# Latent attention: the low parts of the later queries and keys are subtracted on GpSimd instead of VectorE, between its key-sum additions

## The reference, cut to what matters

```python
q = (rms_norm(c_q, g_cq) @ w_uq).reshape(b, l, MLA_HEADS, MLA_QK)      # 64 + 32 columns a head
kv = (rms_norm(c_kv, g_ckv) @ w_ukv).reshape(b, l, MLA_HEADS, MLA_NOPE + MLA_V)
k = jnp.concatenate([k_nope, k_rope], axis=-1)
q = rope_tail(rms_norm(q, g_q_mla), cos, sin)
k = rope_tail(rms_norm(k, g_k_mla), cos, sin)
o_mla = blocked_causal_attention(pad_front(q), pad_front(k), pad_front(v_mla), MLA_QK ** -0.5)[:, PAD:]
```

## Time and profile before

| | us |
|---|---|
| median of 3 runs | 1716.3 |
| lowest and highest of them | 1715.48 and 1719.96 |
| the profiled execution, its own time | 1712.75 |
| span of the profiled execution | 1710.6 |
| TensorE busy | 1657.1 (97% of the span) |
| VectorE busy | 885.7 (52%) |
| ScalarE busy | 624.3 (36%) |
| GpSimd busy | 174.1 (10%) |

### The profile page before, as it was taken

One profiled execution on the slowest core, in us unless ns is written; L12 is line 12 of the kernel. 1 busy time (PEld: TensorE's weight loads), 2 busy tenths in 40 slices (PEclk: granted clock), 3 DMA queues, 4 the chain that ended last, 5 costly groups with the idle time before them and its releaser, 6 DMA issues.

```text
span 1710.6 us, 28146 instructions
## 1 busy us (share of the span) xinstructions
PE 1657.1 (97%) x11861; PEld 1438.5 (84%) x11861; DVE 885.7 (52%) x1148; ACT 624.3 (36%) x954; POOL 174.1 (10%) x146
## 2 busy tenths in 40 slices
PE   7999989999999999999999999999999999897998
PEld 6997767899999999999887888888877788566786
DVE  5544576463343434655566444343466458556554
ACT  5433544333231313221233223232335356554223
POOL 1002202330000000310022000000052000000200
PEclk9999999999999999999999999999999999998999
DMA  6221000132233232223223233222355565001001
GB/s 189 75 75 33 7 28 24 51 99 87 87 99 96 77 98 98 77 96 98 94 79 99 98 99 98 87 89 95 98 117 75 74 99 77 1 1 59 27 27 49
DMA packets 135635, 129.87 MB, mean 76 GB/s; under 512 B 17645, under 2 KB 131428, under 8 KB 135540
## 3 DMA queue, kind: packets, MB, share of 16 engines
q1 hardware_dynamic: 135338, 128.44, 27.1%
q10 hardware_dynamic: 202, 0.06, 0.0%
HBM read 126.39 MB, written 2.10 MB: 75 GB/s over the span
## 4 chain that ended last, share of the span: by engine, by line
PE 92%; DVE 3%; ACT 3%; issue 1%; POOL 1%; SPq 1%; DMA 0%; ACTq 0%; DVEq 0%; POOLq 0%
PE ps L457 72%; PE ps L2195 3%; PE ps L787 2%; PE ps L770 2%; PE ps L1145 1%; PE ps L1966 1%; PE ps L894 1%; PE ps L2329 1%; PE ps L795 1%; PE ps L2318 1%; PE ps L2327 1%; PE ps L1934 0%; PE ps L2353 0%; PE ps L803 0%; SPq L2592 0%
## 5 line engine op out<-in xcount | busy, mean ns | idle before, releaser
L432 ACT ACTIVATE w_hi<-raw 128x1024 fp32r<-128x1024 f32 (+1 forms) x227 | 239.5, 1056 | 805.6 <-PE ps L457 790.1
L457 PE MATMUL ps<-x_hi,w_hi 128*128 128x258 f32 (+4 forms) x1640 | 450.8, 327 | 3.6 <-DVE x_lo L477 2.8
L457 PE MATMUL ps<-x_lo,w_hi 128*128 128x258 f32 (+4 forms) x1640 | 444.6, 323 | 0.0
L457 PE MATMUL ps<-x_hi,w_lo 128*128 128x258 f32 (+4 forms) x1640 | 443.6, 323 | 0.0
L439 DVE TENSOR_TENSOR w_lo<-raw,w_hi 128x1024 fp32r<-128x1024 f32 (+1 forms) x227 | 296.4, 1306 | 97.6 <-ACT w_hi L432 97.6
L457 PEld LDWEIGHTS ps<-x_hi,w_hi 128*128 128x128 f32 (+2 forms) x1640 | 273.5, 188 | 34.7 <-issue 3.8
L457 PEld LDWEIGHTS ps<-x_lo,w_hi 128*128 128x128 f32 (+2 forms) x1640 | 272.5, 188 | 28.1 <-issue 2.4
L457 PEld LDWEIGHTS ps<-x_hi,w_lo 128*128 128x128 f32 (+2 forms) x1640 | 272.3, 188 | 25.8
L457 PE MATMUL ps<-a_hi,w_lo 128*128 128x258 f32 (+1 forms) x960 | 255.1, 320 | 0.0
L457 PE MATMUL ps<-a_hi,w_hi 128*128 128x258 f32 (+1 forms) x960 | 254.9, 320 | 0.0
L457 PE MATMUL ps<-a_lo,w_hi 128*128 128x258 f32 (+1 forms) x960 | 254.8, 320 | 0.0
(11 more groups left out here) (432 smaller groups left out, 1809.9 us busy)
## 6 DMA issues: line engine op xcount, KB each, us to landing
raw<-in_w_mlp_up SPq DMA_DIRECT2D x32, 1024.0 KB, 5.3
raw<-in_w_mlp_down SPq DMA_DIRECT2D x32, 1024.0 KB, 5.1
raw<-in_w_in SPq DMA_DIRECT2D x16, 1024.0 KB, 8.7
raw<-in_w_in_conv SPq DMA_DIRECT2D x12, 1024.0 KB, 5.1
raw<-in_w_in_attn SPq DMA_DIRECT2D x8, 1024.0 KB, 5.1
raw<-in_w_out_attn SPq DMA_DIRECT2D x4, 1024.0 KB, 5.1
raw<-in_w_out_conv SPq DMA_DIRECT2D x4, 1024.0 KB, 5.1
raw<-in_w_out SPq DMA_DIRECT2D x4, 1024.0 KB, 5.3
```

Source lines behind the costliest of these rows:

```text
L432: act.activation(split_tile(w_hi, t), raw_tile(t), ACT.Copy).then_inc(w_hi_ok, 1)
L457: ins = pe.matmul(pair_of_banks[t % 2][0:m, b, 0:c], w[:, k, :], x[:, k, x0:x0 + c], start=(k == order[0] and n == 0), stop=(k == order[-1 ...
```

## The change

Nine subtractions of 128 partitions by 528 columns leave VectorE's order and stand in GpSimd's: three each (plain and rotary columns of the queries, plain columns of the keys) for the operands 1, 2 and 3. Those of operand 0 stay on VectorE, and so do the two subtractions of 32 partitions for the rotary keys (`rope_k_one`) of every operand. The three of operand 1 stand behind GpSimd's last clearing; those of operands 2 and 3 stand between the additions of the stages 4 and 5. GpSimd's work is counted by one semaphore, `fx["added"]`, and the list `pool_work` gives each piece its number; TensorE waits for the piece `("k", c - 4)` ahead of `("s", c, 3)` of the pairs 5, 6 and 7. Every addition now also waits for the piece before it.

```diff
+        pool_work = [("add", c, j) for c in range(4) for j in (1, "end", 2, 3)]
+        pool_work += [("q", 1), ("rope_q", 1), ("k", 1)]
+        for c in range(4, 8):
+            pool_work += [("add", c, 1), ("add", c, "end")] + ([("q", c - 2), ("rope_q", c - 2)] if c < 6 else [])
+            pool_work += [("add", c, 2)] + ([("k", c - 2)] if c < 6 else []) + [("add", c, 3)]
+        def pool_count(*what):
+            return pool_work.index(what) + 1
...
-                    pe.wait_ge(mq["lo"], 2 * (c - 3))
+                    pe.wait_ge(mq["lo"], c - 2)
+                    if c > 4:
+                        pe.wait_ge(fx["added"], pool_count("k", c - 4))
...
-            pe.wait_ge(fx["added"], 4 * c + 4)
+            pe.wait_ge(fx["added"], pool_count("add", c, 3))
...
             pool.wait_ge(fx["exp"], fox_count("u", c, j))
+            if pool_count("add", c, j) > 1:
+                pool.wait_ge(fx["added"], pool_count("add", c, j) - 1)
...
             mla_k_normed(dve, 1)
-            mla_q_lo(dve, 1)
             mla_k_lo(dve, 1)
...
-                    if c < 6 and i == 1:
-                        mla_q_lo(dve, c - 2)
...
         def mla_k_lo(dve, c):
-            dve.wait_ge(mq["hi"], 5 * c + 3)
-            dve.tensor_tensor(fox_lo[:, 4 + c, :], z[:, 4 + c, :], fox_hi[:, 4 + c, :].bitcast(F32), ALU.subtract)
+            if c == 0:
+                dve.wait_ge(mq["hi"], 3)
+                dve.tensor_tensor(fox_lo[:, 4, :], z[:, 4, :], fox_hi[:, 4, :].bitcast(F32), ALU.subtract)
...
+        def mla_q_lo_pool(pool, c):
+            pool.wait_ge(mq["hi"], 5 * c + 1)
+            pool.wait_ge(fx["added"], pool_count("q", c) - 1)
+            pool.tensor_tensor(fox_lo[:, c, :], z[:, c, :], fox_hi[:, c, :].bitcast(F32), ALU.subtract).then_inc(fx["added"], 1)
+            pool.wait_ge(mq["hi"], 5 * c + 2)
+            pool.wait_ge(fx["added"], pool_count("q", c))
+            pool.tensor_tensor(rq_lo[c][:, :], rq[c][:, :], rq_hi[c][:, :].bitcast(F32), ALU.subtract).then_inc(fx["added"], 1)
+
+        def mla_k_lo_pool(pool, c):
+            pool.wait_ge(mq["hi"], 5 * c + 3)
+            pool.wait_ge(fx["added"], pool_count("k", c) - 1)
+            pool.tensor_tensor(fox_lo[:, 4 + c, :], z[:, 4 + c, :], fox_hi[:, 4 + c, :].bitcast(F32), ALU.subtract).then_inc(fx["added"], 1)
...
+            mla_q_lo_pool(pool, 1)
+            mla_k_lo_pool(pool, 1)
             for c in range(4, 8):
-                add_pair(c)
+                add_keys(pool, c, 1)
+                if c < 6:
+                    mla_q_lo_pool(pool, c - 2)
+                add_keys(pool, c, 2)
+                if c < 6:
+                    mla_k_lo_pool(pool, c - 2)
+                add_keys(pool, c, 3)
```

More of the change, by code:

```diff
@@ L970, in add_keys @@
                 pool.tensor_tensor(sums[:, :, :], prob[:, :, P:SEQ + META], prob[:, :, SEQ + META:928], ALU.add).then_inc(fx["added"], 1)
-                pool.wait_ge(fx["added"], 4 * c + 1)
+                pool.wait_ge(fx["added"], pool_count("add", c, 1))
                 part, p0 = sums[0:META, :, 384:400], prob[0:META, :, 928:944]
             elif j == 2:
-                pool.wait_ge(fx["added"], 4 * c + 2)
                 part, p0 = sums[:, :, 128:400], prob[:, :, 944:1216]
             else:
-                pool.wait_ge(fx["added"], 4 * c + 3)
                 part, p0 = sums[:, :, 256:400], prob[:, :, 1216:1360]
@@ L1793, in program @@
                                                ("max", 32), ("exp", 32), ("pv", 8), ("shift", 8), ("out_hi", 8), ("out_lo", 8))}
-        finished.update({"o_unit": (fx["added"], 32), "o_two": (fx["o_done"], 8), "o_sum": (fx["inv"], 8), "o_one": (fx["meta_out"], 8), "o_sq": (fx["meta_max"], 8),
+        finished.update({"o_unit": (fx["added"], len(pool_work)), "o_two": (fx["o_done"], 8), "o_sum": (fx["inv"], 8), "o_one": (fx["meta_out"], 8), "o_sq": (fx["meta_max"], 8),
                          "l2_sq": (fx["squares"], KC), "raw": (mq["raw"], 8), "cleared": (mq["cleared"], 11), "rot_a": (mq["sin"], 5),
```

## The result

The changed kernel takes **1720.97 us** (median, 1718.86 to 1726.89) and the kernel before 1715.48 (1714.87 to 1719.96) in the same comparison. The ratio is 1.0033, with a 95% interval of 1.0025 to 1.0041. That is 5.5 slower, somewhere between 4.3 and 7.0. The forecast of "within 0.3%" was missed narrowly: the median difference is 5.5, the bound was about 5.1, and the interval of 4.3 to 7.0 has that bound inside. The direction of all three terms was right, but their sum of 1.9 was too small by nearly a factor of three.

A forecast was written before the change was run, and what follows sets the result against it. TensorE was taken to bound the kernel, busy 97% of the span with 92% of the chain. Terms of 1.24 + 0.4 + 0.3 gave +1.9, so 1718.2; the range was 1715.6 to 1719.9 with 1.5 of scatter on either side.

The forecast's parts named there:

- three terms: Delays at the scores of pair 5, in stage 4 and in stage 5: 1.24 + 0.4 + 0.3 = 1.94.
- Part 1: Ahead of the scores of pair 5: GpSimd's subtractions of operand 1 end late, so TensorE starts at 260.44, +1.24.
- the forecast's 0.7 to 1.3: Expected sign: TensorE idle this long ahead of the first scores of pair 5, ended by GpSimd.
- the clock rival: New idle at 259.20 brings another 3.3 at half TensorE clock, costing about 1.65; sum +3.6, 1719.9; chance 0.10.
- A clock of 0.5 after 259: Sign named as proving the forecast wrong: TensorE's granted clock at 0.5 past 259 in the profile after.
- Part 2: Stage 4: L992 waits for GpSimd's addition of 544 columns, delaying transpose L862 and all behind, +0.4.
- Part 3: Stage 5: L992 waits for GpSimd's addition of 544 columns, so L862 starts at 285.65, +0.3 instead of -0.72.
- the gain of 0.72: Stage 5: with two subtractions off VectorE, transpose L862 could start at 284.62 instead of 285.34.
- Part 4: The rest: at most some 0.05 where TensorE waits for GpSimd's first additions; later stages and everything else unchanged.
- Taking turns: GpSimd and VectorE operations with two SBUF inputs exclude each other for whole instructions; rival without this: +0.3, 1716.6, chance 0.17.
- GpSimd's price: One moved subtraction costs 1.32 on GpSimd, within 1.05 to 2.16, with 0.07 between instructions.
- cheap and dear rivals: A GpSimd subtraction costs 1.05 (sum -0.7, 1715.6, chance 0.10) or 2.16 (sum +7.5, 1723.8, chance 0.07).

The follow-up runs named there:

- The early placing: Against the kernel before: only operand 1's three subtractions on GpSimd, its two query ones ahead of the clearings; 1715.15, ratio 0.9995.
- operand 1 alone: Against the kernel before: only operand 1's three subtractions on GpSimd, behind its clearings; 1722.32, ratio 1.0036.
- reordered: Against the change: operand 1's query subtractions ahead of the clearings, 544-column addition before the queries, last addition after L1001 in stages 4 and 5; 1716.39, ratio 1.0002.
- The middle wait: Against the kernel before: GpSimd clears a buffer five times and the scores of pair 5 wait for the last; 1718.56, ratio 1.0017.
- the addition held back: Against the change: operand 1 back on VectorE, GpSimd's addition of 544 columns waits for L1001 in stages 4 and 5; 1718.50, ratio 1.0013.
- operands 2 and 3 alone: Against the change: operand 1's three subtractions back on VectorE, the six of operands 2 and 3 stay on GpSimd; 1718.46, ratio 1.0013.
- seven clearings: Against the kernel before: GpSimd clears a buffer seven times and the scores of pair 5 wait for the last; 1724.10, ratio 1.0048.
- two clearings: Against the kernel before: GpSimd clears a buffer twice and the scores of pair 5 wait for the last; 1716.37, ratio 1.0009.

## Why the prediction was off

**The result's direction and the places were right.** The three terms are where they were put, and each has the named cause. Their sizes were too small, 1.94 against 4.60. The time forecast, 1718.2, missed by less than the difference did (2.8 against 3.6), because it started from a median of 1716.3 where the comparison has 1715.48. That is luck.

**Part 1 failed by its size: +3.14 where it said +1.24.** Three things went into it.

1. *The slack was read from a slow trace.* The sum set GpSimd's ready time against 259.20, the start of the scores in before's trace. But TensorE had come through 3.3 at clock 0.50 just ahead, and it was late by 5.45 - 4.04 = 1.41 for that. The early placing (4.04) shows, to about 0.1, the time it wants at full clock. Before's slow stretch hid 1.4 of GpSimd's lateness in the sum. In a trace where the stretch isn't there, that of operand 1 alone, the wait is 3.10. The change's own wait of 1.07 lies in the forecast's 0.7 to 1.3 only because TensorE was slow and late there too.
2. *The ready time was 0.57 early.* Forecast 260.44 - 253.75 = 6.69, measured 7.26, 7.26 and 7.28. Counted from the start of the turned scores, the second subtraction was forecast at 256.3 + 1.39 - 253.75 = 3.94 and came at 258.56 - 254.32 = 4.24: +0.30, the 0.48 behind the first one. The signal to TensorE took 261.58 - 261.32 = 0.26, where 0.04 was counted: +0.22. The pitch of 1.46 instead of 1.39, with 1.30 instead of 1.32 for the last one, gives the other 0.05.
3. *The scores ran at half clock.* From their start to the maximum it took 2.88, where before took 1.55: +1.33. This was the clock rival, which had a chance of 0.10 and a price of 1.65. The argument against it, "1.02 idle before 285.34 cost no clock", was one row of another place. A clock of 0.5 after 259 was also among the prediction's own signs of being wrong, and it is there. All four traces in which the scores wait until 7.26 or later show 0.50 or 0.51 over them.

Item 2 and item 3 together with the forecast's 1.24 give 1.24 + 0.57 + 1.33 = 3.14, against before's trace. Item 1 says that this trace is not the fair comparison by itself, but it happens to come out alike: the seven traces without a wait have the maximum at 5.70, 5.70, 7.00, 7.09, 7.11, 8.54 and 8.54, mean 7.10, and the three with operand 1 late have it at 10.14, 10.14 and 10.16. The difference is 3.05. In the first kind the slow stretch differs from trace to trace, for no reason that the runs show. In the second the late scores cost first the wait and then the clock.

What is shown: a late operand 1, by subtractions or by clearings, reproduces the loss of part 1 in the trace. An early one removes it where operands 2 and 3 are on VectorE (0.9995) or reordered (1.0002), but not where the rest is as in the change (1.0026): there the wait went and a slow stretch came. What is not settled is when the scores run slowly, and so whether the late operand is the cause of the 1.33. The middle wait had them at 1.00. With operand 1's queries ahead of the clearings and the rest as in the change the stretch over them ran at 0.52, with no idle time ahead, and with the addition held back there was one of the same kind (0.54 from 256 to 263, TensorE busy throughout).

**Part 2: +0.99 where it said +0.4.** The mechanism gave +0.52 where it stood alone (operands 2 and 3), an L1001 of 0.68. In the change GpSimd stood idle 5.05 for the queries' high part until 268.81, which is 4.35 after VectorE's first maximum, against 265.76 - 261.88 = 3.88 with operands 2 and 3 alone. So the addition began only 0.22 ahead of L1002, and L1002 was held for nearly all of it (1.13). The other 0.47 appears only together with part 1. That it comes from the clock (0.50 until 265.9) is only inferred from these rows and wasn't tried by itself.

**Part 3: +0.47 where it said +0.3.** Right, and the collision was full (1.32) as expected. Most of the difference comes from GpSimd's pitch: it started the addition at 289.02, 2.92 after the first subtraction at 286.10, where 2.78 was counted (281.36 to 284.14). That the gain of 0.72 was there and was eaten by the collision is shown by the reordered kernel.

**Part 4 and the sums** were right: no wait at L907, nothing after the transpose of pair 6.

**Taking turns** was right. The Trainium skill, SBUF — State Buffer, section "SBUF: two separate sides", has the lock held for a whole instruction; the rows 271.95 and 289.05 of VectorE agree: two columns took 1.13 and 1.32. Also, VectorE's 32 partitions (`rope_k_one`) held up a subtraction of 128, which took 1.79 instead of 1.32. That is 0.47 more, where `rope_k_one` still had 0.63 to run (256.30 to 256.93); no run tells why it is not all of the 0.63.

**GpSimd's price** was right: 1.29 to 1.33 undisturbed. The estimate from the Trainium skill's GPSIMD Engine Reference, sections 1 and 2.1, was 1.10, and the measurement decides against it. The cheap and dear rivals are both out.

**The end.** The trace differences sum to 4.60 and the medians differ by 5.5; 4.60 lies within the interval of 4.3 to 7.0. For the experiment with seven clearings the two do not agree: its stretch is 3.86 longer, and its ratio of 1.0035 to 1.0061 means 6.0 to 10.5. A part of this lies behind the start of the output projection, in code that no experiment touches. From there to the end of the span before's trace takes 1393.4. It is 1395.0 to 1395.2 in both traces of the change, in that of operand 1 early and alone, and in that of two clearings. It is 1397.1 to 1397.4 with operand 1 alone, with operands 2 and 3 alone, with seven and with five clearings, and with the queries early and the rest as in the change. With operand 1 alone, for instance, TensorE's granted clock is 0.50 from 323.80 to 327.10, right behind that start and with the engine busy throughout; before and the change have 1.00 over the whole of the first 14 us. So the ratios of these experiments are more than the price of the place that was changed, and the lengths of the stretch (+3.15, +1.12, +3.86, +0.94 and +2.55 in this order) measure it better. Each is one trace, and whether the later slow stretch follows from the shift in time or from chance is open.

No version measured here beats the kernel before: the early placing of operand 1 (0.9995) and the reordered nine (1.0002) equal it.

## What to carry to other kernels

Read how late an operand may come from executions at full clock: a slow stretch ahead of the consumer hides a lateness that costs its full size at another time, and a new wait there can be followed by slow work. Work moved to a slower, idle engine should go into that engine's idle time well ahead of its consumer; here three subtractions directly in front of the scores cost 3.1 in the trace, and with two of them ten earlier nothing. And look which tiny operation of the critical path takes turns with the moved work: two columns on VectorE went from 0.16 to 1.3.

## What the hardware showed that I had not expected

- When each of GpSimd's operations waits for the one before, the pitch is 1.46 for an operation of 1.31, 0.15 apart. Between additions with less to wait for it was 0.07.
- A subtraction that met VectorE's `rope_k_one` took 1.79 to 1.81, and where another followed (the change, operand 1 alone) it waited 0.48 more. With the addition held back a subtraction that met `rope_k_one` took 1.65, and the addition behind it started after 0.14. Where the 0.48 goes, no run tells.
- Clearings of GpSimd met the same VectorE work and kept to their 3.48 for six.
- The clock at 0.50 covered between nothing and 10.2 at the same place of the program, in kernels with the same TensorE order, with the engine busy throughout or not.
